# Expert loop on TensorE: one choice of column class for each round in place of one for each half

## What is computed

```python
for e in range(N_EXPERTS):                  # 16
    hdn = jax.nn.silu(t @ w1[e]) * (t @ w3[e])    # 1024 -> 512, twice
    out = out + gate[:, e:e + 1] * (hdn @ w2[e])  # 512 -> 1024; gate is 0 for most tokens
```

## Time and profile before

| what | value |
|---|---|
| median of 3 runs | 755.19 us (754.88 to 757.26) |
| the profiled execution's own time | 757.21 us |
| its span, first to last instruction | 755.5 us |
| TensorE busy, matmuls | 719.9 us, 95% of the span |
| TensorE busy, weight loads (beside the matmuls) | 624.4 us |
| DVE, ACT, POOL busy | 426.2, 323.8, 135.9 us |
| mean granted TensorE clock | 0.988 of full speed |
| expert rounds 0 to 15 | about 292.7 to 658.9 us of the span |

### The profile page before, as it was taken

The page is one execution under the profiler, slowest core; times in us unless marked ns, Lnnn a source line. Parts: engine busy times, 40 slices in busy tenths (PEclk is TensorE's granted clock), DMA queues, the critical chain, the costliest instruction groups (busy, mean ns, idle before and its releaser), DMA issues.

```text
span 755.5 us, 12056 instructions
## 1 busy us (share of the span) xinstructions
PE 719.9 (95%) x4420; PEld 624.4 (83%) x4421; DVE 426.2 (56%) x728; ACT 323.8 (43%) x592; POOL 135.9 (18%) x168
## 2 busy tenths in 40 slices
PE   2999999999999988999999999999999999899996
PEld 2887787787888866999988988999999999848885
DVE  4987986894654477234542342444454444467664
ACT  5617659672402234233441332443444333484243
POOL 3655204241001003000000000000000000043420
PEclk9999999999999998999999999999999999999998
DMA  9909934402215176779997695799999999363212
GB/s 323 296 1 294 271 82 153 168 1 84 111 72 200 64 279 217 280 257 346 339 349 258 226 356 192 290 332 362 352 341 336 330 338 366 141 207 116 94 45 85
DMA packets 78288, 169.11 MB, mean 224 GB/s; under 512 B 7580, under 2 KB 19304, under 8 KB 78248
## 3 DMA queue, kind: packets, MB, share of 16 engines
q1 hardware_dynamic: 70112, 141.53, 53.2%
q0 software_dynamic: 4448, 14.62, 6.1%
q10 hardware_dynamic: 3688, 12.43, 4.3%
HBM read 144.51 MB, written 24.05 MB: 223 GB/s over the span
## 4 chain that ended last, share of the span: by engine, by line
PE 94%; issue 1%; ACT 1%; DVE 1%; ACTq 1%; POOL 1%; POOLq 0%; DVEq 0%
PE bank L726 35%; PE bank L937 32%; PE bank L715 5%; PE bank L946 4%; PE bank L948 4%; PE bank L947 4%; PE bank L857 3%; PE bank L707 3%; PE bank L915 2%; PE bank L958 1%; PE bank L955 1%; ACTq L1134 1%; ACT ring_r L426 1%; DVE regN L1425 0%; POOL small L589 0%
## 5 line engine op out<-in xcount | busy, mean ns | idle before, releaser
L726 PE MATMUL bank<-ring_r,regT_r 128*128 128x512 f32 (+1 forms) x648 | 161.5, 384 | 3.1 <-DVE regT_r L1534 1.7
L726 PEld LDWEIGHTS bank<-ring_r,regT_r 128*128 128x128 f32 x648 | 117.9, 188 | 28.6 <-issue 3.4
L937 PE MATMUL bank<-regT,ring 128*128 128x128 f32 (+1 forms) x1024 | 125.6, 284 | 2.4 <-issue 1.8
L937 PEld LDWEIGHTS bank<-regT,ring 128*128 128x128 f32 x1024 | 123.6, 194 | 4.8 <-issue 4.6
L937 PE MATMUL bank<-regN,ring 128*128 128x128 f32 (+1 forms) x1024 | 123.2, 281 | 0.1
L937 PEld LDWEIGHTS bank<-regN,ring 128*128 128x128 f32 x1024 | 122.1, 191 | 1.1 <-issue 0.5
L631 POOL DMA_INDIRECT regT<-n_scratch,idsi x17 | 16.0, 942 | 311.3 <-PEq L904 203.3
L726 PE MATMUL bank<-regT_r,ring_r 128*128 128x256 f32 (+1 forms) x256 | 65.1, 343 | 2.9 <-DVE ring_r L434 2.9
L1746 DVE TENSOR_TENSOR regR<-regR,bank 128x256 f32<-128x256 f32 x32 | 13.5, 422 | 92.2 <-ACT regR L1256 91.9
L1256 ACT ACTIVATE regR<-bank 128x320 f32<-128x320 f32 x32 | 13.8, 432 | 95.9 <-PE bank L937 95.9
L726 PEld LDWEIGHTS bank<-regT_r,ring_r 128*128 128x128 f32 x256 | 45.2, 194 | 8.3 <-issue 3.1
(11 more groups left out here) (311 smaller groups left out, 1240.8 us busy)
## 6 DMA issues: line engine op xcount, KB each, us to landing
ring<-in_w_exp_down SPq DMA_DIRECT2D x16, 2048.0 KB, 15.9
ring<-in_w_exp_gate SPq DMA_DIRECT2D x16, 2048.0 KB, 9.4
ring<-in_w_exp_up SPq DMA_DIRECT2D x16, 2048.0 KB, 16.7
ring<-in_w_in SPq DMA_DIRECT2D x4, 2048.0 KB, 10.8
y_scratch<-zeros SPq DMA_DIRECT2D x4, 1408.0 KB, 12.7
y_scratch<-regN ACTq DMA_DIRECT2D x11, 384.0 KB
h<-in_x_sample SPq DMA_DIRECT2D x8, 512.0 KB, 10.5
y_scratch<-zeros SPq DMA_DIRECT2D x4, 1024.0 KB, 10.7
```

Of the source, the lines that this page charges most:

```text
L726: q = nc.tensor.matmul(out, a, b, start=(n == 0), stop=(n == len(passes) - 1))
L937: q = nc.tensor.matmul(bank[b][:, col:col + n], slot3(s)[:, k, f * P:(f + 1) * P], moe["xT", par][:, k, 0:n], start=(k == 0), stop=(k == K ...
```

## The change

The choice of class is made once for each round. Both halves, the waits for their inputs and the transposes between and after them now stand in each of the two arms. The wait for the previous round's hidden values (hid_done), which stood ahead of each half's choice, moves into the arms too. The instructions that a round executes are otherwise the same, in the same order. Each arm holds 64 + 4 + 64 + 4 matmuls and transposes with a weight load each, where an arm held 64 with theirs. The surplus round has no transposes in its arms.

```diff
@@ -979,23 +979,23 @@
                 pe.wait_ge(t_drained, 3 * (turn_next[1] if turn_next else r + 1))
                 pe.wait_ge(ring_in[sg], loads[0])
                 pe.wait_ge(ring_in[su], loads[1])
-                for half in range(2):
-                    if prev_hidden is not None:
-                        pe.wait_ge(hid_done, 2 * prev_hidden + half + 1)
-
-                    def body(n, half=half):
+                def both_halves(n):
+                    for half in range(2):
+                        if prev_hidden is not None:
+                            pe.wait_ge(hid_done, 2 * prev_hidden + half + 1)
                         hidden(2 * half, par, n)
                         hidden(2 * half + 1, par, n).then_inc(gu_full, 1)
-                    by_size(count, body)
-                    if turn_next:
+                        if not turn_next:
+                            continue
                         if half == 0:
                             pe.wait_ge(gathered[1 - par], turn_next[2])
                             pe.wait_ge(further[1 - par], turn_next[2])
                             if prev_hidden is not None:
-
                                 pe.wait_ge(ylo_drained, 2 * r)
                                 pe.wait_ge(y2_summed, r)
                         turn(half, 1 - par, turn_next[1])
+
+                by_size(count, both_halves)
                 pe.wait_ge(down_low_done, 8 * (r + 1))
```

## The result

The changed kernel is slower: 762.80 us (median of 4 runs, 761.46 to 763.78) against 755.04 for the kernel before (median of 4, 753.96 to 757.26). The ratio is 1.0099, 95% interval 1.0082 to 1.0116. The page of the changed kernel shows the same work as before: the same number of matmuls and loads, the same 26 packets of q8 in the whole execution, and TensorE's share of the chain that ended last 3 points lower.

What follows compares the result with a forecast made beforehand. The prediction took TensorE to bound the kernel and summed 0 (choice) + 0 (moved waits) + 0 (fetch) onto the median of before, forecasting 755.2 us, range 753.6 to 757.4.

Steps and rivals of the forecast that it cites:

- The bound: Whole kernel: TensorE, busy 719.9 of 755.5 us and 94% of the last chain, so only its time counts.
- the choice: Start of each round's second half: dropping the second choice of class gains 0, within bounds of 0 to 5.8 us.
- the moved waits: Waits now written inside both arms: each round passes the same ones in the same order, so 0.
- the losses at the back edges: TensorE's idle time where the loop jumps back to a round's start: 0.36 us, expected to stay.
- The added code: Longer arms, jumped over in rounds 0 to 3: new fetch misses taken as 0, bounds 0 to 14.8 us.
- rival A: Rounds 0 to 3, likeliest round 1's start: first-pass jump lands in unfetched code; 758.9 us for one miss, 762.6 for two; chance 0.07.
- The price of a miss: An uncovered instruction fetch, priced at the loop's exit: 2.5 us idle plus 1.2 us of low clock, 3.7 us.
- the hole at the loop's exit: Jump over the surplus-round block after the loop: 2.53 us idle, expected to stay near 2.5 us.
- The cover at an arm's end: Rounds 0, 2 and 3: the jump at an arm's end comes with hidden matmuls still queued; cost taken as 0.
- Rival B: Looped rounds: the loop leaves the chip or every long jump fetches anew; 790.6 us, 807 with slow clock; chance 0.01.

Runs made afterwards that it cites:

- loop_merged: The changed form only in the loop (rounds 2 to 15), two choices kept in rounds 0 and 1, against the kernel before: 756.27 us, ratio 1.0022.
- merged_spread112: The changed kernel with expert-stage code moved by 112 semaphore increments, spread behind early products: 765.57 us, ratio 1.0145 to the kernel before.
- merged_spread160: The changed kernel with expert-stage code moved by 160 semaphore increments, spread behind early products: 762.17 us, ratio 1.0099 to the kernel before.
- merged_spread208: The changed kernel with expert-stage code moved by 208 semaphore increments, spread behind early products: 762.03 us, ratio 1.0092 to the kernel before.
- merged_wide_first: The changed kernel with its two arms in the other order, the wide one first: 765.50 us, ratio 1.0128 to the kernel before.
- first_merged: The changed form only in written-out rounds 0 and 1, two choices kept in the loop, against the kernel before: 762.94 us, ratio 1.0116.
- merged_shift16: The changed kernel with 16 increments of an unused semaphore at the start of TensorE's program: 763.90 us, ratio 1.0116 to the kernel before.

## Why the prediction was wrong

**The bound, the choice, the moved waits: right.** TensorE's own stream sets the time, half 1 still starts right behind the transposes, and the losses at the back edges are unchanged (0.36 before, 0.39 after). The second choice was worth 0, as read from the earlier trace rows. The estimate from the Trainium skill (Advanced Engine Details and Errata, Control Flow Timing), 2.5 us of gain from 108 and 51 ns, has nothing in any row for it.

**The added code: this is the step that failed.** The prediction said of new misses: "Bounds: 0 to 4 x 3.7 = 14.8 us. I take 0." It reasoned that ten fetches had caused no hole, and that a jump at the end of an arm comes with matmuls queued. Both are observations about jumps over 128 instructions. They say nothing of jumps over more than a packet, which is the one thing that the change made new. By the theory, a jump over 128 that crosses into the next packet of 256 leaves at least about half of it before the one behind is needed; a jump over 272 left 11 instructions here. It is rival A, at the very place it named, the start of round 1, and it deserved far more than 0.07. The range ended at 757.4 and so left it out.

**The price of a miss: too small.** The 3.7 us came from the earlier trace rows, where the DMA queues were almost idle. In round 1, with 351 GB/s moving, the hole was 5.5 and the clock took 1.6: 7.1 for one miss. By the rival's own sum with that price, 755.2 + 7.1 = 762.3 us, and 762.80 was measured. The row was the nearest of its kind, but its surroundings weren't those of the place to be priced. Its 1.2 us of low clock isn't part of every such hole either: in the changed kernel the hole at the loop's exit is 2.46 us long, and the 24 matmuls behind it ran at full clock, in 10.56 us.

**The cover at an arm's end: half right.** No hole shows at those of rounds 0, 2 and 3 in the changed kernel; but the cover failed in loop_merged (1.9 us), merged_spread112 (1.9), merged_spread160 (1.9 in round 0), merged_spread208 (2.6) and merged_wide_first (1.3).

**Rival B: refuted as thought.** No q8 packet in the rest of the loop, in spite of jumps over 272 instructions in every round. The Trainium skill (Runtime: NRT & Kernel Launch, Instruction fetch mechanics) lets a taken branch outside a window of two blocks force a fetch. For code that is already on the chip these rows don't show that: the loop needed about 6 packets and was read once. For code that isn't, they fit one packet ahead.

**Open.** No version that beats the kernel before came out of this. The miss at the loop's exit is in all of them. I didn't try to fill it. Behind its 24 matmuls the transposes already wait 1.2 us for DVE in the changed kernel, so that I expect little from it; no run shows that.

## What to carry to other kernels

Count the instructions that a conditional skips, not only those that it runs. An arm longer than a fetched packet (256 instructions here; each of the 32 float32 matmul calls of a half stands in the trace as two matmuls with two loads) can cost several microseconds the first time through, and at one and the same place more with full DMA queues (5.3 us against 3.1). Merging choices can pay only where the choice itself leaves a gap in the start-to-start distances; here it left none. A hole in the middle of a straight run of instructions, with no semaphore and an instruction packet inside it, points to a fetch; moving the code by a known number of instructions tests it, for the hole moved by as many here (5 matmuls, none with 16 more instructions, 29 with 208 more).

## What the runs showed of the hardware that I had not expected

- Instructions seem to be fetched one packet ahead and in the order of the code, jumped-over packets too: 26 q8 packets in the kernel before and in the changed one. All that I could date in rounds 0 to 3 fit this order, though I inferred the rule from holes and didn't measure it by itself.
- A packet of 16 KB, small beside the 2048 KB of a weight load, cost 5.3 to 6.3 us of idle time at the start of round 1 with 310 to 350 GB/s moving (after, first_merged, merged_shift16), 3.1 us there at half of that, 2.5 at the loop's exit with 80. The packet itself took 1.1 us at either traffic; from its end to TensorE's next instruction it was 1.33 to 1.59 us in all 16 new holes.
- 128 semaphore increments at the start of TensorE's program delayed its first matmul by 10.1 us. The trace has each of them: they start 0.15 us apart, from 0.92 to 20.3 us, so that they outlast the wait for the first tile, which ended at about 10 us. 16 of them are over by 3.4 us (merged_shift16) and cost nothing. Spread four at a time behind queued matmuls they cost nothing that shows.
- The releaser that a row names for a hole can be a bystander: in three rows (loop_merged, merged_spread112, merged_spread160) it was the DVE instruction that happened to end last before TensorE went on.
